# Moving the experts' tokens and rows by indirect transfers bounded by the counts

## The reference

```
logits = h @ w_router + b_router
top_v, top_i = top_k(logits, 2)            # two experts for each token
gates = softmax(top_v)
out = sum over e of gate[e] * (silu(h @ w_in[e]'s gate half) * (h @ w_in[e]'s up half)) @ w_out[e]
```

## Time and profile before

| | |
|---|---|
| median of 3 runs | 1927.91 us (1926.93 to 1933.36) |
| profiled execution | 1925.69 us |
| its span, first to last instruction | 1924.2 us |
| PE (TensorE matmul) busy | 1698.4 us, 88% |
| DVE (VectorE), ACT (ScalarE), POOL busy | 371.7, 316.4, 102.1 us |
| mean granted TensorE clock | 0.958 |
| bytes moved | 529.72 MB, mean 275 GB/s |
| queue q1 (weights; issued by SyncE) | 496.67 MB, 71.5% of 16 DMA engines |
| queue q0 (issued by POOL) | 31.00 MB, 4.9% |
| chain that ended last | PE 71%, DMA 17%, SyncE's queue 6% |

### The profile page before, as it was taken

How to read it: one execution, slowest core, us unless ns; L and a number is a source line. 1 busy time by engine, 2 the same in 40 slices (tenths; PEclk the granted TensorE clock), 3 DMA queues, 4 the chain that set the end, 5 groups by cost and what they waited for, 6 DMA issues and landing times.

```text
span 1924.2 us, 28942 instructions
## 1 busy us (share of the span) xinstructions
PE 1698.4 (88%) x12294; PEld 1183.9 (62%) x12294; DVE 371.7 (19%) x1127; ACT 316.4 (16%) x942; POOL 102.1 (5%) x179
## 2 busy tenths in 40 slices
PE   5998989999999997978999977699999699997772
PEld 3556666667777745767985534299536399463431
DVE  2134333230000225642100101001002011010102
ACT  2223333220000123721000100000001000010002
POOL 1013110000000001001001000000000100001001
PEclk8999999999999996987999999999999899999997
DMA  9545878484435678254888999998769999999992
GB/s 346 177 143 184 309 284 279 172 263 131 133 100 140 220 211 259 81 218 151 305 306 316 396 396 387 403 387 326 262 206 394 399 386 350 325 383 401 387 402 94
DMA packets 260112, 529.72 MB, mean 275 GB/s; under 512 B 8426, under 2 KB 67482, under 8 KB 259843
## 3 DMA queue, kind: packets, MB, share of 16 engines
q1 hardware_dynamic: 248402, 496.67, 71.5%
q0 software_dynamic: 11568, 31.00, 4.9%
HBM read 506.13 MB, written 21.50 MB: 274 GB/s over the span
## 4 chain that ended last, share of the span: by engine, by line
PE 71%; DMA 17%; SPq 6%; DVE 2%; ACT 2%; issue 2%; POOL 0%; POOLq 0%; DVEq 0%
PE ps L1347 16%; PE ps L1223 9%; PE ps L1329 8%; PE ps L1406 8%; PE ps L806 8%; DMA big<-in_w_moe_in 7%; DMA big<-in_w_moe_out 5%; PE ps L866 3%; SPq L621 2%; PE ps L1244 2%; SPq L625 2%; DMA big<-in_w_ada 2%; PE ps L772 1%; DMA work<-in_w_moe_out 1%; PE ps L968 1%
## 5 line engine op out<-in xcount | busy, mean ns | idle before, releaser
L1347 PE MATMUL ps<-big 128*128 128x128 f32 (+1 forms) x2432 | 287.8, 281 | 13.6 <-DMA big<-in_w_moe_in 8.3
L1347 PEld LDWEIGHTS ps<-big 128*128 128x128 f32 x2432 | 286.2, 194 | 14.6 <-issue 14.6
L1329 PE MATMUL ps<-big 128*64 128x256 f32 x1920 | 221.1, 386 | 39.5 <-DMA big<-in_w_moe_in 36.2
L1329 PEld LDWEIGHTS ps<-big 128*64 128x64 f32 x1920 | 137.8, 139 | 116.8 <-DMA big<-in_w_moe_in 39.2
L1223 PE MATMUL ps<-work,big 128*128 128x288 f32 x704 | 171.1, 406 | 2.7 <-ACT work L1513 2.7
L1513 ACT ACTIVATE gqkv<-ps 128x144 f32<-128x144 f32 (+1 forms) x238 | 67.6, 310 | 608.0 <-PE ps L1347 310.7
L1223 PEld LDWEIGHTS ps<-work,big 128*128 128x128 f32 x704 | 133.6, 190 | 39.7 <-issue 2.9
L2362 DVE TENSOR_TENSOR z<-ps,gqkv 128x256 f32<-128x256 f32 x224 | 69.0, 334 | 455.2 <-ACT gqkv L1513 455.2
L1386 PE MATMUL ps<-big,z 128*64 128x512 f32 x496 | 113.1, 598 | 31.6 <-DMA big<-in_w_moe_out 31.5
L1406 PE MATMUL ps<-big,z 128*128 128x512 f32 x288 | 130.8, 601 | 1.4 <-DVE z L2362 1.4
L1513 ACT ACTIVATE work<-ps 128x288 f32<-128x288 f32 (+3 forms) x100 | 40.3, 438 | 360.7 <-PE ps L806 134.5
(11 more groups left out here) (335 smaller groups left out, 1548.1 us busy)
## 6 DMA issues: line engine op xcount, KB each, us to landing
big<-in_w_moe_in SPq DMA_DIRECT2D x98, 2048.0 KB, 19.7
big<-in_w_moe_out SPq DMA_DIRECT2D x49, 2048.0 KB, 20.5
big<-in_w_ada SPq DMA_DIRECT2D x24, 2048.0 KB, 9.5
work<-in_w_moe_in SPq DMA_DIRECT2D x14, 2048.0 KB, 19.8
big<-in_w_ffd_in SPq DMA_DIRECT2D x22, 1024.0 KB, 7.9
work<-in_w_moe_out SPq DMA_DIRECT2D x7, 2048.0 KB, 24.1
big<-in_w_ffd_out SPq DMA_DIRECT2D x8, 1408.0 KB, 7.0
big<-in_cache_b_k SPq DMA_DIRECT2D x4, 2048.0 KB, 7.8
```

The costliest lines, as they stand in the source:

```text
L1329: last = mm(ps[64 * a:64 * a + 64, 512 * b + 256 * g:512 * b + 256 * g + 256], hsel[:, k, 0:NARROW], w[:, k, 256 * a:256 * a + 256], start ...
L1347: last = mm(bank(b, cols, 256 * g), w[g][:, k, 128 * i:128 * i + 128], hsel[:, k, 0:cols], start=(k == 0), stop=(k == KD - 1))
```

## The change

The trash region, the three offsets and the register loads go. VectorE computes, for each expert and each partition, the row (or half, quarter or eighth of a row) of the table that the partition loads or stores; where the count says that the row does not exist, 2^20 is added. POOL moves everything by indirect transfers with a bound on the index, which leave out an index beyond it: two loads and three stores per expert. The token buffers are cleared once. The columns that VectorE needs stand in the constants (88 more). The last expert's load is of the second pass' first tokens, none of which exist if there is one pass. The second pass on POOL is written out for eight experts where it was a loop. Cut to its core:

```diff
-TRASH = (NE + 1) * ROWS
-STORES = 7
+NROWS = NE * ROWS
+FAR = float(1 << 20)
+STORES = 3
+MIDDLE = NARROW
...
+C_AT = C_EPS + 1
+C_TOK = C_AT + 2 * 5 * NE
+NCST = C_TOK + 8
...
-            for i, m in ((0, 10), (10, 10), (20, 9)):
+            for i, m in ((0, 8), (8, 8), (16, 8)):
...
-            def tokens_in(row):
-                gp.dma_start(xtk, rows[bass.ds(row, P), :]).then_inc(e_tok, 16)
-                gp.dma_start(xtk_rest, rows[bass.ds(row + P, EXTRA), :].rearrange("r (k c) -> k r c", k=KD)).then_inc(e_tok, 16)
-            def rows_out(row, row1, col1, row2):
-                gp.dma_start(rows[bass.ds(row, 64), 0:512], o_half[0][0:64, :]).then_inc(e_st, 16)
-                gp.dma_start(rows[bass.ds(row1, 64), bass.ds(col1, 512)], o_half[0][64:128, :]).then_inc(e_st, 16)
-                gp.dma_start(rows[bass.ds(row2, P), 512:1024], o_half[1]).then_inc(e_st, 16)
-                for c in range(4):
-                    gp.dma_start(rows[bass.ds(row + P, EXTRA), 256 * c:256 * c + 256], o_rest[32 * c:32 * c + EXTRA, :]).then_inc(e_st, 16)
+            def tokens_in(again, e):
+                for i, dst, src in ((0, xtk, rows), (1, xtk_rest, eighths)):
+                    gp.indirect_dma_start(dst, None, src, rows_at(place_i[:, again, i, e:e + 1]),
+                                          bounds_check=src.shape[0] - 1, oob_is_err=False).then_inc(e_tok, 16)
+            def rows_out(again, e):
+                for i, dst, src in ((3, halves, o_half[0]), (2, halves, o_half[1]), (4, quarters, o_rest)):
+                    gp.indirect_dma_start(dst, rows_at(place_i[:, again, i, e:e + 1]), src, None,
+                                          bounds_check=dst.shape[0] - 1, oob_is_err=False).then_inc(e_st, 16)
...
             for e in range(NE):
                 gp.wait_ge(e_gat, e + 1)
-                tokens_in((e + 1) * ROWS)
-                row1, col1, row2 = offset(e, NE * ROWS - 64), offset(NE + e, 512), offset(2 * NE + e, TRASH)
+                if e + 1 < NE:
+                    tokens_in(0, e + 1)
+                else:
+                    tokens_in(1, 0)
+                if e == 0:
+                    gp.wait_ge(off_rdy, 2)
                 gp.wait_ge(e_ocA, e + 1)
                 gp.wait_ge(e_ocV, e + 1)
-                rows_out(e * ROWS, row1, col1, row2)
+                rows_out(0, e)
...
-                with gp.Fori(0, NE) as e:
+                for e in range(NE):
...
+            def load_places(again):
+                beyond(far[:, 0, :], tokens, 0)
+                link(beyond(far[:, 1, :], tokens, 1))
+                row_places(again, 0, 2)
...
             choose_first()
             places()
+            first_load()
             gather_copy(1)
+            other_places()
             first_pass()
```

More of the change, by code:

```diff
@@ L65 @@
 C_EPS = C_CM + 128
-NCST = C_EPS + 1
+C_AT = C_EPS + 1
+C_TOK = C_AT + 2 * 5 * NE
+NCST = C_TOK + 8
 M_A, M_B, M_C, M_SB, M_NA, M_NB = 0, 384, 768, 1152, 1152 + BCOLS, 1152 + BCOLS + 256
@@ L81, in shape_constants @@
     c[:, C_EPS] = EPS
+    p, first = np.arange(P), ROWS * np.arange(NE)[None]
+    q, r, r16, k16 = p // 32, p % 32, p % EXTRA, p // EXTRA
+    for again in range(2):
+        row = first + CAP * again
+        rest = 4 * (row + (P if again else NARROW) + r[:, None]) + q[:, None]
+        at = (row + p[:, None], 8 * (row + P + r16[:, None]) + k16[:, None], 2 * row + 2 * p[:, None] + 1,
+              2 * row + (2 * p if again else 2 * (p % 64) + p // 64)[:, None], rest)
+        for i, a in enumerate(at):
+            c[:, C_AT + 8 * (5 * again + i):C_AT + 8 * (5 * again + i) + 8] = a
+    extra = np.where(r < EXTRA, P + r, NT)
+    for i, a in enumerate((p, P + r16, p % 64, extra, NARROW + r, 2 * p - 2 * (p % 64) - p // 64, 4 * (P - NARROW) + 0 * p)):
+        c[:, C_TOK + i] = a
     pos = [np.arange(128), 128 + np.arange(128), PAST + np.arange(128) % TS]
@@ L310, in build @@
         dest = tail[:, place_at + 80:place_at + 86].bitcast(I32)
-        offf = tail[0:1, place_at + 96:place_at + 136].rearrange("p (w n) -> p w n", w=5)
-        offs = tail[0:1, place_at + 144:place_at + 168].bitcast(I32)
+        col = place_at + 352
+        tokens = tail[:, col:col + 8]
+        wide, of_wide, of_small, far_b = (tail[:, col + 8 * i:col + 8 * i + 8] for i in range(1, 5))
+        far = tail[:, col + 40:col + 80].rearrange("p (i n) -> p i n", i=5)
+        at_f = tail[:, col + 80:col + 120].rearrange("p (i n) -> p i n", i=5)
+        place_i = tail[:, col + 120:col + 200].bitcast(I32).rearrange("p (a i n) -> p a i n", a=2, i=5)
         rt = tail[:, KD * CAP + 2 * NT:2048]
@@ L393, in build @@
         s_zero, z_set, s_place = sem("rows_cleared"), sem("zeros_set"), sem("tokens_placed")
-        dest_rdy, off_rdy = sem("places_ready"), sem("store_offsets_ready")
+        dest_rdy, off_rdy, post_rdy = sem("places_ready"), sem("row_places_ready"), sem("last_post_ready")
         s_back = [sem(f"rows_back{t}") for t in range(3)]
@@ L480, in copy_fill @@
             return copy(kb[:, 512 * f:512 * f + w], bank(5 + n % 3, w))
-        rows = nc.dram_tensor("expert_rows", (TRASH + 96 * 2, D), F32, kind="Internal").ap()
+        rows = nc.dram_tensor("expert_rows", (NROWS, D), F32, kind="Internal").ap()
         block = ctx.enter_context(nc.Block())
@@ L717, in offset @@
-            def offset(i, most):
-                return gp.value_load(offs[0:1, i:i + 1], min_val=0, max_val=most)
+            eighths = rows.rearrange("r (k c) -> (r k) c", k=8)
+            halves = rows.rearrange("r (k c) -> (r k) c", k=2)
+            quarters = rows.rearrange("r (k c) -> (r k) c", k=4)
+            def tokens_in(again, e):
+                for i, dst, src in ((0, xtk, rows), (1, xtk_rest, eighths)):
+                    gp.indirect_dma_start(dst, None, src, rows_at(place_i[:, again, i, e:e + 1]),
+                                          bounds_check=src.shape[0] - 1, oob_is_err=False).then_inc(e_tok, 16)
@@ L730, in _ @@
                 gp.wait_ge(e_gat, NE + 1)
-                tokens_in(CAP)
-                with gp.Fori(0, NE) as e:
+                tokens_in(1, 0)
+                for e in range(NE):
                     gp.wait_ge(e_gat, e + (NE + 2))
-                    tokens_in((e + 1) * ROWS + CAP)
+                    tokens_in(1, min(e + 1, NE - 1))
                     gp.wait_ge(e_ocA, e + (NE + 1))
                     gp.wait_ge(e_ocV, e + (NE + 1))
-                    rows_out(e * ROWS + CAP, e * ROWS + (CAP + 64), 0, e * ROWS + CAP)
+                    rows_out(1, e)
                 gp.wait_ge(e_st, 32 * STORES * NE)
@@ L1503, in _ @@
             pe.wait_ge(y_xs, 1)
-            pe.wait_ge(off_rdy, 2)
+            pe.wait_ge(post_rdy, 1)
             for k in range(KD):
@@ L2314, in places_read @@
                                             op0=ALU.mult, op1=ALU.add)
-                link(V.tensor_scalar(offf[:, 0, :], bank(1, 8, 24, 1), float(NARROW), None, ALU.is_gt))
+                link(V.tensor_copy(tokens, bank(1, 8, 24)))
             def choose_first():
@@ L2330, in places @@
                 V.tensor_copy(dest, destf.rearrange("p w t -> p (w t)")).then_inc(dest_rdy, 1)
[L2331 to L2335, removed]
@@ L2336, in places, with beyond @@
-                link(V.tensor_scalar(row2, row2, float(TRASH), None, ALU.add))
-                V.tensor_copy(offs, offf[:, 2:5, :].rearrange("p w n -> p (w n)")).then_inc(off_rdy, 1)
-                V.tensor_copy(post_last.rearrange("p k (b t) -> p k b t", t=TS), per_batch(coef[:, 3, :, :])).then_inc(off_rdy, 1)
+                V.memset(xtk, 0.0)
+                V.memset(xtk_rest, 0.0)
+            def beyond(out, count, limit):
+                return V.tensor_scalar(out, count, cst[:, C_TOK + limit:C_TOK + limit + 1], None, ALU.is_le)
@@ new lines, in row_places @@
+            def row_places(again, i0, i1):
+                c = C_AT + 8 * (5 * again + i0)
+                at = cst[:, c:c + 8 * (i1 - i0)].rearrange("p (i n) -> p i n", i=i1 - i0)
+                link(V.scalar_tensor_tensor(out=at_f[:, i0:i1, :], in0=far[:, i0:i1, :], scalar=FAR, in1=at, op0=ALU.mult, op1=ALU.add))
+            def load_places(again):
+                beyond(far[:, 0, :], tokens, 0)
+                link(beyond(far[:, 1, :], tokens, 1))
+                row_places(again, 0, 2)
@@ new lines, in store_places @@
+            def store_places(again):
+                if again:
+                    link(beyond(far[:, 2, :], tokens, 0))
+                    V.tensor_copy(far[:, 3, :], far[:, 2, :])
+                    link(beyond(far[:, 4, :], tokens, 3))
+                    row_places(1, 2, 5)
+                    return
+                link(V.tensor_scalar(wide, tokens, float(MIDDLE), None, ALU.is_gt))
+                link(V.tensor_tensor(of_wide, tokens, wide, ALU.mult))
+                link(V.tensor_tensor(of_small, tokens, of_wide, ALU.subtract))
+                beyond(far[:, 2, :], of_wide, 0)
```

(21 more changed lines are left out.)

## The result

The changed kernel takes 1915.39 us (median of 7 runs, 1912.62 to 1923.14) where the kernel before took 1927.91 (7 runs, 1926.37 to 1937.48): 12.5 us less, a ratio of 0.992, 95% interval 0.990 to 0.994. The forecast was 1921.5 us, its range ended at 1916.0; the direction held, but what came is twice the 6.4 us worked out. The profiled executions took 1925.69 us and 1912.62 us, their spans 1924.2 and 1911.0.

What follows compares the result with a forecast made beforehand. Weight transfers and sync issues were taken to bound three stretches, TensorE leading elsewhere. Terms -7.5 (experts), +1.0 (end) and +0.1 (start) gave -6.4 us, so 1919.3 for the profiled execution and 1921.5 us for the median; range 1916 to 1929.

Steps and rivals of the forecast that it cites:

- The sum in the experts' stage: Time saved at the seven expert boundaries by not moving rows that do not exist: 7.5 us.
- A, B and C: Transfer-bound: A (experts 1, 2), B (expert 4), C (6, 7); gaining 2.1 to 4.2, 0.8 to 1.4, 2.7 to 3.9 us.
- the share of q0: Token queue's time in the second and third expert stretch: falls from 3.0 us to 1.3 and 2.0.
- The upper end: Experts' boundaries: the saving goes by bytes not moved over the whole queue, together 9.4 us.
- The lower end: Experts' boundaries: the slowest DMA engine, serving low partitions, decides when a chunk has landed; 5.5 us saved.
- rival 2: Experts' boundaries: every skipped row still costs the queue its turn, so no time is saved; 1929.0 us, chance 0.11.
- The estimated 6.6 us: Experts' boundaries: the slowest-engine sum if each engine serves four partitions and the four lying 32 above.
- The end: After expert 7: the last store lands 3.7 us after its issue, 1.0 us later than before; range -0.8 to +1.0.
- The value set aside, 1.8: After expert 7: the last store, moving nothing, could land 1.8 us after its issue, 0.8 us earlier than before.
- POOL's issue: Each expert: seven stores and two loads become five indirect issues, 6.3 us for 5.0; costs nothing except at the end.
- Rival 3: At the end POOL pays for each of 258 skipped indices; at 60 ns each +15.5 us, 1937 us, chance 0.08.
- Rival 4: Before the final gathers the jump over the unused second pass stalls: up to 3.5 us back, 1925.0 us, chance 0.08.

Runs made afterwards that it cites:

- experiments 3 and 4: Changed kernel plus four 64-row loads at each boundary, on partitions 0 to 63 or on even partitions; experts' stretch 852.9 and 842.4 us, ratios 1.007 and 1.002.
- all_rows: Changed kernel with rows that do not exist loaded and stored too, by the same five transfers; ratio 0.999 to the kernel before, experts' stretch 837.8 us.
- experiment 9: Changed kernel with every first-pass index beyond the bound, so all transfers are issued but move no row; experts' stretch 822.4 us, one execution.
- Experiments 12 and 13: The kernel of experiment 9 plus one 64-row load per boundary, on partitions 0 to 63 or 64 to 127; experts' stretch 827.5 and 828.8 us.
- low_rows: Changed kernel plus four loads of 64 rows at each boundary, on partitions 0 to 63; experts' stretch 852.9 us, ratio 1.007 to the kernel before.
- no_stores: Changed kernel with only the stores' indices beyond the bound, so real rows are loaded but no expert's rows stored; experts' stretch 825.5 us, one execution.
- experiments 8 and 11: Wait for the output's stores moved from POOL to the sync engine, in the changed kernel and the kernel before; ratios 0.990 and 0.996 to the kernel before.
- after_again: Changed kernel run again unaltered, as base for the other runs; 1918.7 us, ratio 0.993 to the kernel before, experts' stretch 827.51 us.

## Why the prediction was wrong, step by step

**The sum in the experts' stage was mis-sized: 10.8 us where 7.5 stood.** The rows as counted, the direction, the split over A, B and C and the share of q0 held. The step that failed is the choice between the two ends ("I take the middle of 9.4 and 5.5"). The upper end was the nearer, and even it was short in C (4.2 us for 3.9) and in B (2.5 for 1.4). Behind experts 2 and 4 it counted the stores alone (the prediction's words: "the loads come too late to delay the pair"). Counted in full, the boundary behind expert 4 gives 3.0 x (1 - 99/288) = 2.0 us, and B then 2.5, as measured; but A by the same count would be 5.0, and it was 4.1.

The lower end was not a wrong mechanism: experiments 3 and 4, 10.6 us apart, show that the place of the bytes counts. But alone it has 5.5 us, and all_rows shows 10.3. What it left out is that existing rows do not pay the full price (experiment 9), so what was taken off was the dear part. A reason is argued, not shown: some part of a chunk is late whatever the rows do, and the first bytes of the rows lie beside that delay. With no row moved at all (no_rows) a chunk's 16 parts still land 2.15 us apart in the median. What makes the late part late no run shows. Experiments 12 and 13 support a price that grows with load on the low half only, and leave the cause open.

Two readings were loose as well. The 1.03 "in every narrow stretch" holds for four of the five; the last shows 0.98 and 369 GB/s. And the 7 us issue behind expert 1, named as a sign of rival 2, stayed under the change without rival 2 being true.

The Trainium skill's partition scheme ("DMA: Bandwidth & Descriptors", "The descriptor swizzle") agrees with experiments 3 and 4 in so far as partitions 0 to 63 are served by half of the engines. The estimated 6.6 us worked out from it was short too.

**The end: +1.0 forecast, -0.3 measured.** The landing was mis-sized: 3.7 us by the earlier trace rows where the last store, which moves no row of expert 7, landed 2.06 us after its issue. The value set aside, 1.8, was the nearer, but partly by luck. Over the 13 profiles with bounded stores the last one landed after 2.1 to 2.4 us in ten and after 3.8 to 4.0 in three (all_rows, low_rows, no_stores). Bytes do not tell the two apart, since no_stores stores nothing; its piece of the chain:

```profile
1875.70 4.04 DMA expert_rows<-work,big
```

What does, no run shows.

**A term was missing: POOL's drain, 2.5 us.** It stood in the trace of before, and I had read the chain only to the last output. It goes by the number of transfers that POOL issued: 4.887 us with 140 (six profiles), 5.459 with 147 (four), 7.174 with 168 (two), 7.502 with 172, which is 82 ns for each more. Packets do not order it: q0 has 14224 in low_rows and 11568 in the kernel before, whose drain is the longer. The change issues 32 transfers fewer. That price and experiments 8 and 11 show the term.

**What held.** POOL's issue, VectorE's operations and the wait for loaded tokens cost nothing that shows: among TensorE's waits in the changed kernel's experts' stage none is for tokens. Rival 2 fell: q0 keeps its count of packets, yet the stretch is 10.3 us shorter than with all rows moved, and with every index skipped the issues behind expert 1 take 5.4 us, so a skipped row does not cost a turn worth seeing. Rival 3 fell: the end did not grow with 258 skipped indices, and all_rows, which skips none, has the same 1.0 us issues. Rival 4 fell: the gap ahead of the gathers' issue is 1.13 us for 0.91, so the jump did not stall. The rule of the Trainium skill ("Runtime: NRT & Kernel Launch", "Instruction fetch mechanics"), by which the target would lie inside the two pages, agrees.

Of the 13.2 us, then, 9 to 10.3 are bytes (all_rows against after_again, with and without the estimated 1.2 us for what all_rows stores on top), 2.2 to 2.6 the drain (experiments 8 and 11; 32 x 0.082), and the rest, 0.3 to 1.9 us, is not told apart.

## What to carry to other kernels

When a stage is bound by transfers, padding that is moved "because it does no harm" costs its bytes (here 10.3 us for 1086 rows): bound indices by the real count, and see on which partitions the remaining rows sit (10.6 us between two layouts of the same bytes). Read the trace past the last result: what an engine does at the very end is on the path, and can often begin earlier by moving a wait to the engine that issued the transfer. When two ends of a bound rest on different mechanisms, a middle of them is no estimate; say which one the rows support.

## What was not expected of the hardware

POOL's closing drain takes 82 ns more for each transfer that POOL issued (4.887 us at 140, 7.502 at 172; nothing outside was run), whatever the transfers moved. Begun early, it lies beside other work. A skipped index leaves q0's packet count unchanged (10192 in both) and costs no time that these runs can see. The same 7.3 MB of additional loads cost 14.8 us over the seven boundaries when spread over all partitions and 25.4 when the lower half of the partitions carried them. A store of nothing, last on its queue, landed after 2.06 us in no_rows and after 4.04 in no_stores.
